# Neighbourhood attention over tokens in column order, two heads a step, two tiles of local keys

## What is computed

```python
# h = 8 heads of dh = 64; 512 tokens are a grid of 8 rows and 64 columns; 256 context tokens beside them
col_start = clip(col - 8, 0, 64 - 16)              # col = 0 ... 63
col_valid = (key_col >= col_start) & (key_col < col_start + 16)
# all 8 rows are in each window
bias = where(col_valid, rpb[head, row_off, col_off], -inf)
s_loc = q @ k.T * 64 ** -0.5 + bias
s_ctx = q @ k_ctx.T * 64 ** -0.5
p = softmax(concatenate([s_loc, s_ctx]))
o = p[:, local] @ v + p[:, context] @ v_ctx
```

## Time and profile before

| what | value |
|---|---|
| median of three runs | 2599.91 us (2598.89 to 2608.19) |
| the profiled execution | 2597.65 us, span 2596.4 us |
| mean granted clock of TensorE | 0.943 |
| PE, DVE, ACT, POOL busy | 2377.0, 1563.3, 926.8, 744.0 us |
| neighbourhood attention, from the first L2198 to the end of the last L2221 | 2028.5 to 2180.7 us |

### The profile page before, as it was taken

One profiled execution on the slowest core, in us unless ns is written; L12 is line 12 of the kernel. 1 busy time (PEld: TensorE's weight loads), 2 busy tenths in 40 slices (PEclk: granted clock), 3 DMA queues, 4 the chain that ended last, 5 costly groups with the idle time before them and its releaser, 6 DMA issues.

```text
span 2596.4 us, 32715 instructions
## 1 busy us (share of the span) xinstructions
PE 2377.0 (92%) x13338; PEld 1392.1 (54%) x13411; DVE 1563.3 (60%) x2634; ACT 926.8 (36%) x1114; POOL 744.0 (29%) x550
## 2 busy tenths in 40 slices
PE   6999888878799998899999999998799888899998
PEld 4566555444465555677656555555354565344443
DVE  2436337233898999999588888888481663433002
ACT  4331226232333333565433333332332444333210
POOL 3310000131141424222233333345154002255540
PEclk7999778999899999899999999999899889999999
DMA  5010642021596877688899999998301101122310
GB/s 179 33 66 33 227 168 92 33 82 40 189 328 229 316 256 286 237 316 308 287 360 380 378 375 375 377 376 307 122 34 65 62 29 55 43 97 98 130 65 33
DMA packets 194503, 484.77 MB, mean 187 GB/s; under 512 B 10742, under 2 KB 93732, under 8 KB 188337
## 3 DMA queue, kind: packets, MB, share of 16 engines
q1 hardware_dynamic: 154624, 334.65, 36.9%
q0 software_dynamic: 39728, 148.03, 15.1%
HBM read 430.21 MB, written 52.43 MB: 186 GB/s over the span
## 4 chain that ended last, share of the span: by engine, by line
PE 52%; DVE 24%; DMA 15%; issue 3%; ACT 3%; POOL 2%; SPq 1%; DVEq 0%; ACTq 0%; POOLq 0%
PE psum L511 12%; PE psum L512 12%; PE psum L513 12%; DMA expert_act<-act_dram 11%; DVE weight_low L1739 6%; PE psum L750 2%; DVE row_sum L1961 2%; DMA rows_b<-peer_v_dram,row_index 2%; PE psum L569 2%; PE psum L862 2%; POOL weight_low L2274 2%; PE psum L658 1%; DVE hidden_low L2127 1%; DMA rows_a<-peer_v_dram,row_index 1%; PE psum L1001 1%
## 5 line engine op out<-in xcount | busy, mean ns | idle before, releaser
L511 PE MATMUL psum<-x_high,weight_high 128*128 128x384 bf16 (+3 forms) x1832 | 641.6, 350 | 41.9 <-DVE weight_low L1739 24.0
L512 PE MATMUL psum<-x_low,weight_high 128*128 128x384 bf16 (+3 forms) x1842 | 644.8, 350 | 20.4 <-DVE x_low L1675 14.8
L513 PE MATMUL psum<-x_high,weight_low 128*128 128x384 bf16 (+3 forms) x1843 | 643.9, 349 | 0.7
L2274 POOL TENSOR_TENSOR weight_low<-weight_stage,weight_high 128x512 bf16<-128x512 f32 (+1 forms) x237 | 313.5, 1357 | 476.1 <-ACT weight_high L1123 476.1
L1123 ACT ACTIVATE weight_high<-weight_stage 128x4096 bf16<-128x4096 f32 (+2 forms) x100 | 356.0, 3562 | 248.3 <-PE psum L513 147.2
L511 PE MATMUL psum<-hidden_high,weight_high 128*128 128x384 bf16 x1024 | 336.1, 328 | 14.5 <-DVE hidden_low L2127 14.4
L512 PE MATMUL psum<-hidden_low,weight_high 128*128 128x384 bf16 x1024 | 336.1, 328 | 0.0
L513 PE MATMUL psum<-hidden_high,weight_low 128*128 128x384 bf16 x1024 | 335.9, 328 | 0.0
L1739 DVE TENSOR_TENSOR weight_low<-weight_stage,weight_high 128x4096 bf16<-128x4096 f32 x69 | 305.7, 4430 | 35.8 <-ACT weight_high L1123 35.8
L511 PEld LDWEIGHTS psum<-x_high,weight_high 128*128 128x128 bf16 (+1 forms) x1856 | 185.7, 100 | 228.2 <-issue 33.1
L513 PEld LDWEIGHTS psum<-x_high,weight_low 128*128 128x128 bf16 (+1 forms) x1856 | 186.0, 100 | 158.2 <-issue 11.3
(11 more groups left out here) (319 smaller groups left out, 3375.8 us busy)
## 6 DMA issues: line engine op xcount, KB each, us to landing
weight_stage<-peer_u_dram SPq DMA_DIRECT2D x32, 2048.0 KB, 9.5
weight_stage<-peer_v_dram SPq DMA_DIRECT2D x32, 2048.0 KB, 11.5
weight_stage<-mlp_w_dram SPq DMA_DIRECT2D x16, 2048.0 KB, 8.0
weight_stage<-ada_w_dram SPq DMA_DIRECT2D x12, 2048.0 KB, 8.0
act_dram<-norm_value SPq DMA_DIRECT2D x128, 192.0 KB, 10.9
gate_dram<-gate_matrices SPq DMA_DIRECT2D x12, 2048.0 KB, 12.8
gates<-gate_dram SPq DMA_DIRECT2D x32, 768.0 KB, 16.5
expert_act<-act_dram SPq DMA_DIRECT2D x32, 768.0 KB, 18.4
```

What stands on the lines that cost most here:

```text
L511: self.nc.tensor.matmul(out, left[0], right[0], start=first, stop=False)
L512: self.nc.tensor.matmul(out, left[0], right[1], start=False, stop=False)
L513: return self.nc.tensor.matmul(out, left[1], right[0], start=False, stop=last)
L2274: ins = nc.gpsimd.tensor_tensor(m.w_low[:, n % SPLITS, at], m.w_stage[:, n % STAGES, at], m.w_high[:, n % SPLITS, at], ALU.subtract)
```

## The change

The tokens of the second block's attention lie column by column (8 rows of a column side by side), so that the 16 columns that a tile of 128 queries can see lie in two tiles of 128 keys; the queries are shifted by half a window (64 tokens), with the first 64 at the end. Steps go by pairs of heads: 16 steps of two heads, 128 queries, 256 local and 256 context keys. The two heads' products alternate, on partitions 0 to 63 and 64 to 127 of the contraction in `scores` and of the output in `applying`. The scale goes into the copy of the queries, the bias is added within PSUM, the exponential reads PSUM. `norm1_2` writes the tokens in column order, reading in strides of 64 elements; the copies of `conv_in` and `fourier_in` and the result of the attention are put back in row order, reading PSUM in strides of 8 elements. The window (now 256 KB) and the first two pairs' biases (512 KB each) are loaded after the Fourier products. The host lays bias and window out accordingly.

The diff, cut to its core; of the functions printed above, replaced lines are left out:

```diff
-GW, ROWS, WC, WR = 64, 8, 16, 8
-NBIAS = 2 * ROWS - 2
+GW, ROWS, WC = 64, 8, 16
+EDGE, LOCAL = ROWS * WC // 2, 2 * P
+NA_LOCAL = ((0, 1), (1, 2), (2, 3), (0, 3))
...
-        self.window, self.bias = m("window", [P, GW]), m("bias", [P, 2, NBIAS, GW])
-        self.na_e, self.na_stat = m("na_exp", [P, 3, KEYS2]), m("na_stats", [P, 2, 8])
+        self.window, self.bias = m("window", [P, 2, LOCAL]), m("bias", [P, 2, 2, 2, LOCAL])
+        self.na_stat = m("na_stats", [P, 2, 8])
+        self.na_e = Map(nc, before_conv)("na_exp", [P, 3, 2, BANK])
...
-NA_STEPS = [(h, t) for h in range(NH2) for t in range(QT)]
+NA_STEPS = [(p, t) for p in range(NH2 // 2) for t in range(QT)]
...
-            self.free_bank(j, (s.mixed, ("na_biased", n)))
-            self.free_bank(j + 1, (s.mixed, ("na_scaled", n)))
...
+            p, t = NA_STEPS[n]
+            keys = m.kt[:, p, 0:SEQ].rearrange("p (a n) -> p a n", n=P)
+            keys = keys[:, t:t + 2, :] if t < QT - 1 else keys[:, 0::QT - 1, :]
+            queries = m.qt[:, p, P * t:P * (t + 1)]
+            for x in range(2):
+                self.free_bank(2 * (n % 2) + x, (s.exped, ("na", n, x)))
+            for part in range(2):
+                for x in range(2):
+                    rows, j = slice(64 * x, 64 * x + 64), 2 * (n % 2) + x
+                    if part == 0:
+                        nc.tensor.matmul(k.bank(j, LOCAL), queries[rows], keys[rows], start=True, stop=True)
+                    else:
+                        ins = nc.tensor.matmul(k.psum[:, j, LOCAL:BANK], queries[rows], m.kt[rows, p, SEQ:KEYS2],
+                                               start=True, stop=True)
+                        ins.then_inc(*s.scored.up("na", n, x))
         def turning(n):
             nc.tensor.wait_ge(*s.mixed.at("na_normed", n))
...
+            for x in range(2):
+                self.free_bank(4 + x, (s.copied, ("na", n)))
+                for y in range(4):
+                    ins = nc.tensor.transpose(k.psum[:, 4 + x, P * y:P * (y + 1)], m.na_e[:, n % 3, x, P * y:P * (y + 1)],
+                                              m.ident[:, :])
             ins.then_inc(*s.turned.up("na", n))
...
+            p, t = NA_STEPS[n]
+            bank, tiles = 6 + p % 2, NA_LOCAL[t] + (QT, QT + 1)
+            nc.tensor.wait_ge(*s.copied.at("na", n))
+            if t == 0:
+                self.free_bank(bank, (s.head_taken, ("na", p)))
+            out = k.psum[:, bank, P * t:P * (t + 1)]
+            for y, tile in enumerate(tiles):
+                for x in range(2):
+                    h, rows = 2 * p + x, slice(64 * x, 64 * x + 64)
+                    ins = nc.tensor.matmul(out[rows], m.vt[:, tile, HD2 * h:HD2 * (h + 1)], et[:, n % 2, x, y, :],
+                                           start=y == 0, stop=y == 3, skip_group_check=True)
             ins.then_inc(*s.applied.up("na", n))
...
+    return m.norm3.value[:, :, :].rearrange("p a (b m) -> p (a b) m", m=P).rearrange("p (v x y) m -> p v x y m", v=2, x=2)
...
-            self.take(("conv_in", g), m.convx[:, g, HALF_TAPS:HALF_TAPS + SEQ])
+            self.take_rows(("conv_in", g), m.convx[:, g, HALF_TAPS:HALF_TAPS + SEQ])
         for g in range(2):
-            self.take(("conv_in", 2 + g), m.gin[:, g, :], func=ACT.Sigmoid)
+            self.take_rows(("conv_in", 2 + g), m.gin[:, g, :], ACT.Sigmoid)
...
-            self.take(("fourier_in", f), m.fin[:, f, :])
+            self.take_rows(("fourier_in", f), m.fin[:, f, :])
...
-            self.take(("q2", f), m.qt[:, f, :])
+            nc.scalar.wait_ge(*s.tile.at("q2", f))
+            nc.scalar.activation(m.qt[:, f, SEQ - EDGE:SEQ], k.tile_bank(("q2", f), EDGE), ACT.Copy,
+                                 scale=HD2 ** -0.5).then_inc(*s.act_out.up("q2_edge", f))
+            nc.scalar.activation(m.qt[:, f, 0:SEQ - EDGE], k.psum[:, k.bank_of["q2", f], EDGE:SEQ], ACT.Copy,
+                                 scale=HD2 ** -0.5).then_inc(*s.act_out.up("q2", f))
+    def take_rows(self, event, dst, func=ACT.Copy):
+        nc, s = self.nc, self.s
+        nc.scalar.wait_ge(*s.tile.at(*event))
+        nc.scalar.activation(dst.rearrange("p (r c) -> p r c", c=GW),
+                             self.k.tile_bank(event).rearrange("p (c r) -> p r c", r=ROWS), func).then_inc(
+            *s.act_out.up(*event))
...
+            st = m.na_stat[:, n % 2, :]
             nc.scalar.wait_ge(*s.score_max.at("na", n))
...
+            if n >= 3:
+                nc.scalar.wait_ge(*s.turned.at("na", n - 3))
+            for x in range(2):
+                nc.scalar.activation(m.na_e[:, n % 3, x, :], k.bank(2 * (n % 2) + x), ACT.Exp, bias=st[:, x:x + 1],
+                                     scale=1.0, accum_out=st[:, 2 + x:3 + x]).then_inc(*s.exped.up("na", n, x))
...
             nc.scalar.wait_ge(*s.turned.at("na", n))
             if n >= 2:
                 nc.scalar.wait_ge(*s.applied.at("na", n - 2))
...
+            nc.scalar.activation(et[:, n % 2].rearrange("p x y m -> p (x y m)"),
+                                 k.psum[:, 4:6, :].rearrange("p x n -> p (x n)"), ACT.Copy).then_inc(*s.copied.up("na", n))
...
+            rows, grid = o.rearrange("p (r c) -> p r c", c=GW), k.bank(6 + pair % 2).rearrange("p (c r) -> p r c", r=ROWS)
+            nc.scalar.activation(rows[:, :, 0:WC // 2], grid[:, :, GW - WC // 2:GW], ACT.Copy).then_inc(
+                *s.head_taken.up("na_edge", pair))
+            nc.scalar.activation(rows[:, :, WC // 2:GW], grid[:, :, 0:GW - WC // 2], ACT.Copy).then_inc(
+                *s.head_taken.up("na", pair))
...
+                ins = (value[:, t % 4, 0:n], x[:, t, 0:n], inverse[:, 0:n])
+                if j == "norm1_2":
+                    ins = (ins[0].rearrange("p (c r) -> p c r", r=ROWS),) + tuple(
+                        y.rearrange("p (r c) -> p c r", c=GW) for y in ins[1:])
+                nc.vector.scalar_tensor_tensor(ins[0], ins[1], gain(t), ins[2], ALU.mult, ALU.mult).then_inc(
+                    *s.normed.up(j, t))
...
+        def masked(p):
+            nc.vector.wait_ge(*s.in_bias[p % 2].at(p))
+            for x in range(2):
+                nc.vector.tensor_tensor(m.bias[:, p % 2, x, :, :], m.bias[:, p % 2, x, :, :], m.window[:, :, :],
+                                        ALU.add).then_inc(*s.masked.up(p, x))
         def scores(n):
...
+            p, t = NA_STEPS[n]
+            st, j = m.na_stat[:, n % 2, :], 2 * (n % 2)
+            local, both = k.psum[:, j:j + 2, 0:LOCAL], k.psum[:, j:j + 2, :]
+            nc.vector.wait_ge(*s.scored.at("na", n, 1))
             if t == 0:
...
+                nc.vector.wait_ge(*s.masked.at(p, 1))
+            nc.vector.tensor_tensor(local, local, m.bias[:, p % 2, :, t // (QT - 1), :], ALU.add).then_inc(
                 *s.mixed.up("na_biased", n))
...
+            nc.vector.wait_ge(*s.mixed.at("na_biased", n))
+            nc.vector.tensor_reduce(st[:, 0:2], both, AX.X, ALU.max, negate=True).then_inc(*s.score_max.up("na", n))
+        def norm(n):
+            st = m.na_stat[:, n % 2, :]
+            nc.vector.wait_ge(*s.exped.at("na", n, 1))
+            nc.vector.reciprocal(st[:, 4:6], st[:, 2:4]).then_inc(*s.step.up())
             nc.vector.wait_ge(*s.step.now())
...
+            for x in range(2):
+                e = m.na_e[:, n % 3, x, :]
+                ins = nc.vector.tensor_scalar(e, e, st[:, 4 + x:5 + x], None, ALU.mult)
+                ins.then_inc(*(s.step.up() if x == 0 else s.mixed.up("na_normed", n)))
...
-        for name in ("conv_in", "fourier_in", "k2", "v2", "q2"):
+        for name in ("conv_in", "fourier_in"):
             self.begin(name)
...
-        nc.gpsimd.wait_ge(*s.act_out.at("q2", 3))
...
+        nc.gpsimd.wait_ge(*s.act_out.at("dft_out", 1))
+        nc.gpsimd.dma_start(m.window[:, :, :], d["window"]).then_inc(*s.in_window.up())
+        for p in range(2):
+            nc.gpsimd.dma_start(m.bias[:, p], d["bias"][p]).then_inc(*s.in_bias[p].up(p))
+        for name in ("k2", "v2", "q2"):
+            self.begin(name)
+        for p in range(2, NH2 // 2):
+            nc.gpsimd.wait_ge(*s.mixed.at("na_biased", QT * (p - 2) + QT - 1))
+            nc.gpsimd.dma_start(m.bias[:, p % 2], d["bias"][p]).then_inc(*s.in_bias[p % 2].up(p))
```

More of the change, by code:

```diff
@@ L1549, in head @@
                 nc.scalar.wait_ge(*s.x_low.at("na", pair - 1))
-            nc.scalar.activation(o, k.bank(6 + pair % 2), ACT.Copy).then_inc(*s.head_taken.up("na", pair))
+            rows, grid = o.rearrange("p (r c) -> p r c", c=GW), k.bank(6 + pair % 2).rearrange("p (c r) -> p r c", r=ROWS)
[3 more added lines that the diff above has]
+                *s.head_taken.up("na", pair))
             nc.scalar.wait_ge(*s.head_taken.at("na", pair))
@@ L2209, in norm @@
-        def norm(n):
-            st, e = m.na_stat[:, n % 2, :], m.na_e[:, n % 3, :]
-            nc.vector.wait_ge(*s.exped.at("na", n))
-            nc.vector.reciprocal(st[:, 3:4], st[:, 2:3]).then_inc(*s.step.up())
```

(40 more changed lines are left out.)

57 lines of the change are left out of this document (5 added, 52 removed).

## The result

| | median of the runs | profiled execution | span | attention |
|---|---|---|---|---|
| before | 2601.05 us (2598.89 to 2608.19, 4 runs) | 2597.65 us | 2596.4 us | 152.23 us |
| after | 2540.28 us (2537.23 to 2542.92, 4 runs) | 2542.35 us | 2541.1 us | 84.57 us |

The changed kernel is faster: the ratio is 0.9759, with a 95% interval of 0.9743 to 0.9775. A second series (E10) gave 0.9751 (0.9735 to 0.9768). "Attention" is, as in the prediction, the time from the first bias addition to the end of the last low part.

What follows compares the result with a forecast made beforehand. It took a loop of waits through VectorE, ScalarE and TensorE in the attention as the bound. Attention 61.1 us less, the stretch before 5.2 more: 2597.65 - 55.9 = 2541.7, with 2.26 a median of 2544 us, range 2531 to 2563.

Steps and rivals of the forecast that it cites:

- The frame: Attention: a loop of waits through VectorE, ScalarE and TensorE over two rounds sets the step, before and after; no engine full.
- The loop: Attention, two steps: TensorE 3.37, VectorE 2.03, ScalarE 2.65 and passing on 0.05 make 8.10 us; 16 steps 64.8 us.
- The rest of the attention: Way in and out, stops, masks, half clock: 24.5 us, plus 2.4 for stops, minus 0.6 for masks.
- the charge for the heads' strided copies: Attention's four stops: two copies, 0.2 us for the second and 0.4 for the PSUM stride, 0.6 each, 2.4 in all.
- Before the attention: Stretch ahead of the first bias addition: masks 0.6, norm 3.2, strided copies 1.2, last q2 0.2, together 5.2 us more.
- The three strided copies: Last copy of conv_in and both of fourier_in: 0.4 us more each, 1.2 in all, from 0 to 1.5.
- The moved loads: POOL, before the attention: three issues, 1.6 us, fit into its idle wait and cost nothing; without that cover 1.6 us.
- Rival 1: Applying is not packed and stays at 1.95 us: 6.0 us more, 2550 us; chance 0.2.
- Rival 2: No packing in scores or applying; TensorE 4.87 us a loop instead of 3.37: 12 us more, 2556 us; chance 0.08.
- Rival 3: TensorE granted 1.2 GHz through the whole attention: 27 us more, some 7 already counted, 2564 us; chance 0.06.
- Rival 4: All open terms low: strides free (6.0 us), products at ideal half (3), less half clock (2): 2533 us; chance 0.06.
- Rival 5: Strided reads on the chain make it slower than before: turns at 8.1 ns an element, 2615 us at 10; chance 0.02.

Runs made afterwards that it cites:

- E10: The changed kernel, unedited, run again on one chip beside the kernel before: median 2537.01 us, ratio to before 0.9751.
- E11: The kernel before, with only ScalarE's copy of the turned scores put ahead of its exponentials: median 2584.1 us, ratio to before 0.9928, attention 135.20 us.
- E8: The changed kernel with window and first biases loaded after the last copy of the queries again: 177.01 us to the first addition, attention 84.67 us.
- E1: The changed kernel with both heads' products of applying on the same 64 output columns: applying 1.89 us instead of 1.02, attention 90.55 us.
- E2: The changed kernel with both heads' scores on partitions 0 to 63: scores 1.94 us instead of 1.11 at full clock, attention 99.74 us.
- E4: The changed kernel with norm1_2 reading and writing packed, in row order: reciprocal to first addition 170.07 us instead of 176.86.
- E5: The changed kernel with norm1_2 reading packed and writing with stride: instruction 1133 ns against 1381, reciprocal to first addition 174.05 us.

## Why the prediction was right, and where it was off

- **The frame** held: the same loop through three engines set the step before and after. The prediction gave 2544 for the median, 2540.28 came; its profiled execution was put at 2541.7 and came at 2542.35. That last agreement is luck: 8.3 us more were gained than the sum said, and the first block of that execution was 8.9 us longer.
- **The loop**, 8.10 forecast, was 7.73 us. Two terms are at fault, each by about 0.17. In TensorE's share, 3.20 for 3.37, it is applying: I took 1.20 between 0.97 and 1.95 and it was 1.02; turning was 1.07 (1.12), scores 1.11 (1.05). ScalarE's share was 2.48 (2.65): the two exponentials 1.42 (1.54), the copy 0.92 (0.99). VectorE's was 2.02 (2.03), with a maximum of 1.24 (1.22). VectorE's addition within PSUM costs nothing extra: 696 ns, as the 0.69 to SBUF. Eight loops give 3.0 us more than forecast.
- **The rest of the attention**, 26.3 forecast, was 84.57 - 8 x 7.73 = 22.7 us. The step at fault is the charge for the heads' strided copies, 0.6 each. The two took 0.12 + 0.44 us at a stop (first fence, changed kernel) where one took 0.50 (second fence, before), so 0.06 each: 2.2 us too much. ScalarE reads PSUM with a stride of 8 for nothing; L1433, a strided write, was the wrong row to go by. The clock gave more than the 1.4 us that remain: the half-clock rows of the chain lie above their full-clock prices by some 13 us in the kernel before and some 9 in the changed one. So other terms go the other way by some 2.6 us, which I have not traced.

```profile
2068.84 0.12 ACT norm_inverse L1580
2068.96 0.44 ACT norm_inverse L1582
```

```profile
2072.00 0.50 ACT norm_inverse L1550
```

- **Before the attention**, +5.2 forecast, +4.7 found. The sum is right by errors that cancel. The norm cost 4.5 us, not 3.2: 0.57 us an instruction on the chain where L2067 suggested 0.4, and the instruction took 1381 ns, not the 1.15 us named as a sign. Another 2.3 us of half clock stood behind it, which I had left out; in E10, the same code, 0.6 of it stood there and 1.8 in the projection `v2`, and the sum was the same. The three strided copies, charged 1.2, cost nothing: 0.98 us for two in both kernels, not about 1.0 each. The last `q2` in two copies cost 0.05 (0.2), the masks 0.5 (0.6). And the execution of before had lost 2.7 us on its way: E11 has its code up to the attention and reached the first addition in 169.51 us, not 172.20. The difference stands in the first products of `v2`, at 0.43 us in before's chain and at 0.22 in E11's. Against E11 the change costs 7.4 there.

```profile
1958.95 0.43 PE psum L512
```

This is a row of the chain of waits of the kernel before, behind POOL's low part that `v2` waits for.

- **The moved loads**, nothing: right, by E8 and the timeline of POOL.
- **Rival 1**, applying not packed, is refuted by the 1.02 us and by E1. The Trainium skill, TensorE: Matmul & The Clock Gate, section "The mechanism", ties the overlap of a weight load to a different row group. Here all rows are used by both heads, the 16 records take 1.02 us, and 1.89 when both heads use the same columns: the measurement decides against that reading.
- **Rival 2**, no packing at all: no; E1 and E2 show that the two packings are worth 0.87 and 0.83 us a round, 1.7 together.
- **Rival 3**, half clock throughout: no; 0.96 in a plain stretch, the same as before, and 0.76 in one with a stop. The share of half clock did grow: 0.84 over the whole attention, where it was 0.89. E2 shows that more of it can come about, for reasons that I had not named.
- **Rival 4**, all open terms low (2533): in part. The strided copies were free and applying was near its ideal half, but the strided reads of the norm cost 4.5 us where it had them free.
- **Rival 5**, the strides: the price of an element was 0.57 us / 512 = 1.1 ns, far from the 8 it needed. The Trainium skill, SBUF — State Buffer, section "Specifications (TRN2)", states a penalty for each crossing to another 16-byte line; E4 and E5 agree with it (747 ns packed, 1133 and 1381 with strides). The strided reads of PSUM, which is not SBUF, showed none.

## What to carry to other kernels

Where a loop passes through several engines, look at the order of the two jobs on the engine between them first: the copy that the matrix engine waits for, put ahead of the exponentials that it doesn't, gave 12.6 us of 84.6 here and 17.0 of 152.2 in the old kernel, for an edit of two lines. How full the engine of the products looks is no guide to it: E11 was expected to give 6 us at most, as TensorE had 3.80 us of work in a step of 3.99. Two products of 64 rows or of 64 columns placed side by side cost about half (0.54 to 0.57), with weight loads as often as every 128 columns. Put strided accesses where ScalarE reads PSUM (free here), not where VectorE reads or writes SBUF on the path.

## What the hardware showed that was not expected

- Long stretches at half clock in which TensorE never stops. In E2 it was busy for 20.60 of the 20.60 us from 2049 at a granted clock of 0.50. The changed kernel was back at full clock some 4 us after its first scores: its first turning, at 2048.92, still took 1.97 us, the scores at 2050.81 took 0.81. The one edit between them is which rows the odd heads' scores use. It is not a matter of that edit alone, though: the kernel before was busy for 11.90 of the 11.90 us from 2115.1 at 0.50, behind a stop. Its chain there is below; at full clock these three took 0.84, 1.46 and 1.05. What ends such a stretch was not followed up.

```profile
2115.07 1.51 PE psum L990 x6
2116.58 2.75 PE psum L1001 x12
2119.33 2.00 PE psum L981 x2
```

- Short stretches at half clock follow a wait of TensorE in one execution and not in another of the same code: behind `norm1_2` 2.3 us in the changed kernel and 0.6 in E10; at `v2` 2.7 us in before and 1.8 in E10, none in E11 and in the changed kernel.
- VectorE's write with 32 bytes between elements: 1133 ns against 747. Its two reads with 256 bytes between them came to 1381: 386 ns more for one strided operand, 634 for two.
- The same code differed by 8.9 us in the first block (before and E11; 17.6 between E1 and E2, whose first block is the same) and by 2.7 us between the reciprocal and the attention (before, E11). A term under some 5 us is read from its own stretch, not from the total.
